# Adding the two experts' rows of a mixture-of-experts layer on TensorE, with diagonal matrices of gates, where VectorE did it in two passes

## What is computed

```
ff = gate_1 * y_1 + gate_2 * y_2                 # the two experts' rows of the token
h  = _layer_norm(DN_ALPHA * h + ff, ln2_g, ln2_b)    # DN_ALPHA = 4 ** 0.25
```

## Time and profile before

| | |
|---|---|
| median of 3 runs (5394.40 to 5401.44) | 5400.27 us |
| the profiled execution: its own time | 5393.46 us |
| its span in the trace | 5391.6 us |
| mean granted clock of TensorE over the span | 0.95 of full speed |
| combine stage of layer 1, first load issued to last `lo` | 1957.98 to 2061.45 us |
| combine stage of layer 2, the same | 3978.25 to 4077.73 us |

### The profile page before, as it was taken

The page is one execution under the profiler, slowest core; times in us unless marked ns, Lnnn a source line. Parts: engine busy times, 40 slices in busy tenths (PEclk is TensorE's granted clock), DMA queues, the critical chain, the costliest instruction groups (busy, mean ns, idle before and its releaser), DMA issues. The chain is left out here.

```text
span 5391.6 us, 128874 instructions
## 1 busy us (share of the span) xinstructions
PE 4819.5 (89%) x56564; PEld 4154.7 (77%) x56564; DVE 3312.1 (61%) x5055; ACT 2134.1 (40%) x3885; POOL 1304.3 (24%) x940
## 2 busy tenths in 40 slices
PE   6989999998799957989999997799957988999999
PEld 5888888886588847878888886588845766788887
DVE  5435665557788864345665557788875465662662
ACT  2323333332188842433333332188843244232331
POOL 0012333332144510012333332144411100122221
PEclk9999999998799977989999998799978989999999
DMA  4420101003366653410101004366652101233332
GB/s 135 140 53 19 32 20 31 19 19 114 119 229 254 251 174 97 124 53 20 31 20 31 19 19 115 120 231 251 251 172 86 39 1 67 90 98 121 110 98 106
DMA packets 383087, 536.31 MB, mean 99 GB/s; under 512 B 136483, under 2 KB 306595, under 8 KB 354467
## 3 DMA queue, kind: packets, MB, share of 16 engines
q1 hardware_dynamic: 339714, 488.61, 28.3%
q0 software_dynamic: 41472, 34.21, 2.1%
q10 hardware_dynamic: 1344, 5.24, 0.3%
HBM read 573.01 MB, written 122.09 MB: 129 GB/s over the span
## 5 line engine op out<-in xcount | busy, mean ns | idle before, releaser
L280 PE MATMUL ps<-w_hi,xbT 128*128 128x512 f32 x1536 | 502.3, 398 | 18.0 <-DVE w L2437 18.0
L280 PE MATMUL ps<-hT,w_in 128*128 128x416 f32 (+1 forms) x2736 | 490.7, 338 | 9.0 <-DVE w_in L761 9.0
L280 PEld LDWEIGHTS ps<-hT,w_in 128*128 128x128 f32 x2736 | 457.3, 195 | 35.3 <-issue 29.3
L2437 DVE TENSOR_TENSOR w<-w,w_hi 128x2048 fp32r<-128x2048 f32 x192 | 429.9, 2278 | 2.2 <-ACT w_hi L2394 2.2
L1486 POOL TENSOR_TENSOR lm<-Ab,consts 116x416 f32<-116x416 f32 x240 | 254.8, 1069 | 592.0 <-PE ps L280 316.4
L2394 ACT ACTIVATE w_hi<-w 128x2048 fp32r<-128x2048 f32 x192 | 359.0, 1935 | 0.0
L280 PEld LDWEIGHTS ps<-w_hi,xbT 128*128 128x128 f32 x1536 | 289.6, 189 | 86.3 <-DVE w L2437 27.1
L280 PE MATMUL ps<-w,xbT 128*128 128x512 f32 x768 | 300.6, 391 | 0.0
L280 PE MATMUL ps<-v,pT 104*104 104x128 f32 (+1 forms) x2176 | 270.3, 280 | 28.2 <-issue 27.4
L2468 DVE TENSOR_TENSOR w<-w,w_hi 128x2048 fp32r<-128x2048 f32 x96 | 223.5, 2328 | 97.0 <-ACT w_hi L2430 97.0
L280 PEld LDWEIGHTS ps<-v,pT 104*104 104x104 f32 (+1 forms) x2176 | 248.8, 178 | 39.9 <-issue 32.4
(11 more groups left out here) (449 smaller groups left out, 11384.9 us busy)
## 6 DMA issues: line engine op xcount, KB each, us to landing
w<-in_moe_w_dram SPq DMA_DIRECT2D x192, 1024.0 KB, 10.0
w_gate<-in_w_gate_dram SPq DMA_DIRECT2D x44, 512.0 KB, 3.9
w_up<-in_w_up_dram SPq DMA_DIRECT2D x44, 512.0 KB, 3.9
w_down<-in_w_down_dram SPq DMA_DIRECT2D x44, 512.0 KB, 3.2
w_in<-in_w_in_dram SPq DMA_DIRECT2D x36, 512.0 KB, 4.3
ys<-t_ys SPq DMA_DIRECT2D x20, 832.0 KB
t_h<-x SPq DMA_DIRECT2D x30, 416.0 KB
w_out<-in_w_out_dram SPq DMA_DIRECT2D x24, 512.0 KB, 7.3
```

Source lines behind the costliest of these rows:

```text
L280: made = e.matmul(out, a, b, start=start, stop=stop)
L2437: e.tensor_tensor(w.lo, w.x, w.hf, ALU.subtract).then_inc(*P.c("moe_dve").tick(li, "w13", b, k))
```

## The change

TensorE forms gate_1 * y_1 + gate_2 * y_2: ScalarE writes, for each tile, two 104 x 104 matrices with the gates of the two experts on the diagonal (the identity times a gate per row), and TensorE multiplies each with its expert's rows, 512 columns at a time, accumulating the two products in a PSUM bank. That is four plain float32 matmuls for a tile. VectorE adds 4 ** 0.25 * h and the sum in two instructions of 512 columns that read the banks. ScalarE's scaling pass over h is gone. The banks are divided anew: 0 to 3 hold the transposes (reused every second tile), 4 to 7 the sums (the same). In TensorE's order the sum of tile i+1 stands ahead of the transposes of tile i.

```diff
@@ combine_mem
     m.tmp = [P.region(16, "stat") for _ in range(NS)]
+    m.diag = [P.region2(2, C, "diag") for _ in range(2)]
@@ combine_part
-    return s, columns(P.ps[2 * (i % 4) + half], C)[:, :, skip:C]
+    return s, columns(P.ps[2 * (i % 2) + half], C)[:, :, skip:C]
+
+
+def combine_sum(P, i, half):
+    return P.ps[4 + 2 * (i % 2) + half][0:C, :]
@@ combine_act
         i = t[0]
         if i is not None:
-            x = m.hx[i % NS][0:C, :]
-            e.wait_ge(*P.d(f"com_{i % NS}_in").at(li, i, "h"))
-            e.activation(x, x, ACT.Copy, scale=ALPHA1).then_inc(*ac.tick(li, i, "h"))
+            if i >= 2:
+                e.wait_ge(*P.c("com_pe").at(li, i - 2, "sum", 1))
+            for kx in range(2):
+                e.activation(m.diag[i % 2][0:C, kx, :], P.K["ident"][0:C, 0:C], ACT.Copy, scale=P.gates[0:C, kx, i:i + 1]
+                             ).then_inc(*ac.tick(li, i, "diag", kx))
@@ combine_dve
             x = m.hx[i % NS][0:C, :]
-            e.wait_ge(*ac.at(li, i, "h"))
-            for kx in range(2):
-                if kx:
-                    e.wait_ge(*dv.last())
-                e.scalar_tensor_tensor(x, m.yv[i % NS][0:C, kx, :], P.gates[0:C, kx, i:i + 1], x, ALU.mult, ALU.add
-                                       ).then_inc(*dv.tick(li, i, "y", kx))
+            e.wait_ge(*P.d(f"com_{i % NS}_in").at(li, i, "h"))
+            for half in range(2):
+                xh = x[:, 512 * half:512 * half + 512]
+                e.wait_ge(*P.c("com_pe").at(li, i, "sum", half))
+                e.scalar_tensor_tensor(xh, xh, ALPHA1, combine_sum(P, i, half), ALU.mult, ALU.add
+                                       ).then_inc(*dv.tick(li, i, "y", half))
@@ combine_pe
+    def add(i):
+        for half in range(2):
+            if i >= 2:
+                e.wait_ge(*P.c("com_dve").at(li, i - 2, "y", half))
+            if half == 0:
+                e.wait_ge(*P.d(f"com_{i % NS}_in").at(li, i, "h"))
+            for kx in range(2):
+                e.wait_ge(*P.c("com_act").at(li, i, "diag", kx))
+                made = e.matmul(combine_sum(P, i, half), m.diag[i % 2][0:C, kx, :],
+                                m.yv[i % NS][0:C, kx, 512 * half:512 * half + 512], start=kx == 0, stop=kx == 1)
+            made.then_inc(*pe.tick(li, i, "sum", half))
+
+    add(0)
     for i in range(NT):
+        if i + 1 < NT:
+            add(i + 1)
         combine_norm(P, li, i).done(e)
         for half in range(2):
-            b = 2 * (i % 4) + half
-            if i >= 4:
-                e.wait_ge(*P.c("com_dve").at(li, i - 4, "lo", half))
-            psv = columns(P.ps[b], C)
+            if i >= 2:
+                e.wait_ge(*P.c("com_dve").at(li, i - 2, "lo", half))
+            psv = columns(P.ps[2 * (i % 2) + half], C)
```

## The result

The change made the program slower: median 5428.24 us of 4 runs (5427.6 to 5434.91) beside 5399.22 us of 4 runs of the kernel before (5394.4 to 5401.44), ratio 1.0054 with a 95% interval of 1.0038 to 1.0070. That is 29.0 us, and more than the 0.2% that counts as a difference here. It lies above the range that was given (5385 to 5410). The profiled execution has a span of 5425.8 us, before 5391.6.

The account below looks back on a forecast made before the run. VectorE was taken to set the pace in the two combine stages. High-clock gains of 5.6 and 8.4 us make 14.0, less 8.5 for clock falls leaves 5.5: 5400.3 - 5.5 = 5394.8, rounded 5395 us; range 5385 to 5410.

Parts of the forecast that it names:

- VectorE, 2.64 to 1.32: Combine stages: two 512-column bank passes replace two of 1024 columns, 2.64 to 1.32 us; VectorE's own tile 8.53 to 7.21.
- The sum on TensorE, 3.44 or 6.84, and 0.2 of tail: Four float32 matmuls per tile add 3.44 us at the high clock or 6.84 at the low, plus 0.2 tail.
- The ring: From one tile's statistics over diagonals and sum to the next statistics: 7.25 us at the high clock, 10.7 at the low.
- The sum without the clock, 14.0 us: Total gain of both combine stages at the high clock: 5.6 us in the first, 8.4 in the second, together 14.0.
- Transfers: Combine-stage loads and stores, 1.70 MB per tile, taken as just hidden; at the same rate no tile under 7.8 us.
- The rest: The normed tile, the fence and all other stages stay untouched.
- the clock's term, "5 x 1.7 = 8.5": TensorE's clock in the combine stages swings; five falls at 1.7 us each cost 8.5 us; chance 0.47.
- grant 0.93 after a burst of 2.8 us: Trace row: a 2.8 us burst between idle stretches preceded a 0.93 grant for 3.4 us; cited for a high clock.
- B: Clock low in most tiles, VectorE waiting for the sum's second half; 5412 with one fall per sum, 5435 without rise; chance 0.18.
- A: TensorE's clock stays high from the second tile on; gain 14.0 us, so 5386; chance 0.15.
- C: Transfers set the combine stages' pace, 7.8 us per tile instead of 7.25; gain 3 to 8 us, 5392 to 5397; chance 0.12.
- D: Nothing measurable: VectorE's gain is used up by unseen waits, within 3 us of before; chance 0.08.

Follow-up runs that it names:

- e2: The changed kernel with the sums' operands read as rounded float32, one pass instead of four, less exact; stages 188.34 us, program ratio to before 0.9976.
- e3: The changed kernel with the diagonals written one tile earlier, ahead of square root and `hi` copies, in a third buffer; stages 198.02 us, ratio to before 0.9997.
- e5: The changed kernel with diagonals one tile earlier and two unused filling matmuls ahead of each sum from tile 2 on; stages 195.20 us, ratio to before 0.9979.
- e1: The changed kernel with two unused float32 matmuls of 512 columns ahead of each sum from tile 2 on; stages 196.17 us, ratio to before 0.9994.
- e4: The kernel before with one part of the change alone, transposes in two pairs of banks instead of four; stages 202.72 us, ratio to before 1.0013.
- e6: The changed kernel with one unused filling matmul ahead of each sum from tile 2 on; stages 202.22 us, ratio to before 0.9994.
- e7: The kernel before with four more unread matmuls of 512 columns per tile ahead of the transposes; stages 203.03 us, ratio to before 0.9990.

## Why the prediction was wrong

**What held.**

- *VectorE, 2.64 to 1.32.* The two bank passes take 1.28 us and 1.31 start to start in e2; VectorE's own tile is 7.20 (7.21 forecast), seen in e2, e3 and e5.
- *The sum on TensorE, 3.44 or 6.84, and 0.2 of tail.* Eight records take 3.65 at the high clock and at most 6.94 (at 4022.04) where the grant is low for nearly all of them. The two diagonals take 0.65 us.
- *The ring.* Drawn rightly, with every wait in its place. At the high clock it is 7.50 instead of 7.25, 0.2 of it in the step from the statistics to the first matmul (M + 1.55 for M + 1.35). At the low clock 10.7 was given (its own terms, M + 1.35 + 6.84 + 0.2 and 2.25 behind it, add up to 10.64); tile 3 took 10.46 or 10.47 in both stages, the steady ones 10.25, since the last microsecond of the sum is fast again.
- *The sum without the clock, 14.0 us,* as a size only. e2, in which the clock has no grip, gained 14.6 in the stages (7.0 and 7.6; 5.6 and 8.4 were forecast), but its sum takes 2.00 us and stands off the ring, and its tile is 7.20. The float32 sum kept high from tile 2 on (e1) has a ring of 7.50 and gained 6.8.
- *Transfers.* Hidden in after (a DMA share of 0.55 and 0.66). That they are only just hidden at 7.2 us is right as well: in the second stage of e2 eight of ten sums start with their load, and in e3 eleven of the twelve from tile 4 on.
- *The rest.* The banks cost nothing (e4), and no other part of the path moved.

**What failed: the clock's term, "5 x 1.7 = 8.5".** The prediction said that the clock would go up and down, and it did, in a pattern of 3.4 us high and 6.8 us low: in the tile shown it fell to 0.50 at about 4062.8, 1.2 us ahead of the sum, and was back by 4069.6, 0.9 us ahead of the sum's end. Both factors were wrong.

The count was five, two at the waits for tile 4 and three in the ten tiles behind. The runs show a fall in nearly every tile: 18 of 20 sums took 5.8 us or more, and of the ten behind tile 4 eight ran low and one in part. The prediction had the idle time in hand (2.9 us per tile, measured 3.13) beside a row where a gap of 3.0 us was followed by a grant of 0.53, and it then treated the fall as an exception that strikes a few tiles. The ring makes a pattern of it: the gap belongs to the ring itself (statistics, square root, `hi` copies, diagonals) and comes back in each tile, whatever the sum takes. That is what e1 shows. It filled a part of the gap and changed nothing else on the ring, and the falls were gone from all steady tiles.

The price was 1.7 us, half of 3.4 us of dense work, which holds if the grant comes back during the sum. It comes back when the sum is all but over, and so is spent on transposes and on idle time. The price is the difference between the two rings, 10.25 - 7.50 = 2.75 us. The row of the forecast with grant 0.93 after a burst of 2.8 us was read as a sign that a burst brings the clock back early; here most of a sum of 6.4 us is over before it comes.

Set against e2, where the sum is off the ring, after is 40.6 us longer in the stages, and the two prices account for it. The ten tiles (five in each stage) from M of tile 4 on are 26.5 us longer (47.6 and 51.4 beside 36.0 and 36.4). At 10.25 - 7.20 = 3.05 each they would be 30.5, less 2.75 for the one tile that kept the clock and 1.1 for the one that lost it half-way: 26.6. The tiles from M of tile 1 to M of tile 4 are 11.8 longer, 8.4 in the second stage, where three tiles at 3.05 would be 9.1, and 3.3 in the first, where e2 waits for tile 4's load as well (its sum begins at 2007.96, after 11.58 us of idle time). The first two tiles are 2.3 longer. With the 14.6 that e2 gained on before, 40.6 - 14.6 = 26.0 is the loss.

**The rivals.** B had the mechanism and the place (the wait of the successor of L2606 for the second half of the sum) and was given 0.18, with two prices. The end with one fall per sum, 5412, used the same 1.7 and was 16 us short; the other end, no rise at all, gave 5435, 7 above the measured 5428. What it cited against itself, that 6.84 us is longer than the stretch after which one row was back at 1.00, is true of this ring too and doesn't help: the grant is back 0.9 us ahead of the sum's end. A (5386, 14 below before) took for granted what e1 and e5 had to make by filling the idle time: e1 is 0.8 below before on its chip, and e5, which also has the diagonals early, 12.2 below, of which its stages account for 7.8. C is not seen in after; with the diagonals early (e3) the loads are what TensorE waits for. D is excluded by VectorE's waits.

The Trainium skill ("TensorE: Matmul & The Clock Gate", A second HAM failure mode: psum-queue depth-cycling) tells of a swing from short idle times at a cost in throughput. The traces agree in kind, with a sum of 6.44 us beside transposes at the high clock in each tile.

**Two prices.** Of the 10.25 us, 7.20 is VectorE's part, 0.30 the wait for the diagonals at the high clock (the step from e1 to e5), and 2.75 the clock (gone in e1 and e5, and in e2 by way of the shorter sum). They can't simply be taken off one by one: the early diagonals alone (e3) bring the mean of the ten tiles behind tile 4 from 9.89 to 7.80 us, 2.1 and not 0.30, as only four of the ten sums run low there and one of the four costs nothing.

**What stays open.** Why one tile of after kept the clock: the sum at 2019.71 has the same 3.13 us of idle time ahead of it as its neighbours that lost it, and the one difference seen is that it follows the wait of tile 4. Whether an earlier load would give back the 5 us of tile 4 was not tried. Why e4's program reads 0.13% slower with equal stages is not settled either.

## What to carry to other kernels

When work moves to TensorE inside a ring that another engine paces, write down the engine's idle time per turn, and look in the trace for what a gap of that size did to the clock; a gap that the ring repeats makes the fall a part of every turn, and its price is the difference between the ring at the two clocks, not a share of one burst. Price the ring at the low clock first and ask whether it still wins: a sum short enough for that (e2, less exact), or operands ready ahead of the ring together with matmuls that fill its gap (e5), turned a loss of 0.54% into a gain of 0.2%. Once the ring is short, look at what each sum waits for next; here it was the load. And a stage that ran at 0.50 before tells nothing, good or bad, as long as TensorE is off its ring; the same 0.50 is 27% of the tile once it is on it (2.75 of 10.25 us).

## What the runs showed of the hardware

- The granted clock and a kernel's ring can run in step: in after 3.4 us at 1.00 and 6.8 us at 0.50 in each 10.25 us, with the low part on all but the last microsecond of the sum.
- More work made the stages 33 us shorter: two unused matmuls per tile (1.88 us at the high clock) hold the grant at 1.00 in the steady tiles of e1.
- By idle time ahead of the sum, twelve sums each: 1.41 us no fall (e1), 2.27 us four (e6), 3.13 us eleven, one of them in part (after). In e7, with gaps of 4.15 and 2.47 us in turn ahead of the transposes, the sets took 4.74 and 3.60 us.
- From the last update of a load's semaphore to the first matmul that waits for it: 0.09 us, in eleven sums of e3. From the end of ScalarE's first copy to the matmul that waits for it: 0.14 us (e1).
- Two bank-reading passes of 512 columns on VectorE take the time of one pass of 1024 with all operands in SBUF, 1.28 us both (L2613 twice and L323); the bank as an operand adds nothing that the trace shows.
